# Two attentions with the order of TensorE's work turned round in every other step

## The reference

```
def chunk_attention(q, k, v, rel_bias):          # "second attention", a == 1; head size 64
    ...
        s = jnp.einsum('bqhd,bkhd->bhqk', qch, kb, preferred_element_type=jnp.float32) * scale + bias[None]
        s = jnp.where(valid[None, None, None, :], s, NEG_INF)
        p = jax.nn.softmax(s, axis=-1).astype(vb.dtype)
        return jnp.einsum('bhqk,bkhd->bqhd', p, vb)

def mla_attention(q, k, v):                      # "third attention", a == 2; query and key size 96, value size 64
    ...
        s = jnp.einsum('bqhd,bkhd->bhqk', qi, k, preferred_element_type=jnp.float32) * scale
        s = jnp.where(mask[None, None], s, NEG_INF)
        p = jax.nn.softmax(s, axis=-1).astype(v.dtype)
        return jnp.einsum('bhqk,bkhd->bqhd', p, v)

    x = x + g_a[:, None, :] * jnp.dot(jnp.concatenate([o_mla, o_ca], axis=-1), w_out[l])
```

## Time and profile before

| | |
|---|---|
| median of 3 runs | 1185.09 us (1184.55 to 1185.25) |
| the profiled execution | 1185.58 us, of which the span from the first to the last instruction is 1183.9 us |
| PE busy | 1175.9 us, 99% of the span |
| DVE, ACT, POOL busy | 585.2, 507.9, 454.7 us |
| granted TensorE clock | 9 tenths or more in each of the 40 slices |
| second attention, steps 0 to 19 | about 662 to 708 us from the span's start |
| third attention, steps 0 to 19 | about 727 to 780 us |

### The profile page before, as it was taken

How to read it: one execution, slowest core, us unless ns; L and a number is a source line. 1 busy time by engine, 2 the same in 40 slices (tenths; PEclk the granted TensorE clock), 3 DMA queues, 4 the chain that set the end, 5 groups by cost and what they waited for, 6 DMA issues and landing times.

```text
span 1183.9 us, 16147 instructions
## 1 busy us (share of the span) xinstructions
PE 1175.9 (99%) x5972; PEld 962.0 (81%) x5972; DVE 585.2 (49%) x1150; ACT 507.9 (43%) x794; POOL 454.7 (38%) x181
## 2 busy tenths in 40 slices
PE   9999999999999999999999999999999999999998
PEld 7887778988888888888988667689888888888887
DVE  4276455877777774212574567835434334340000
ACT  6452453634434442322646576834534443432110
POOL 6352224344344433444443210314434434434442
PEclk9999999999999999999999999999999999999999
DMA  8233122545554542223341110202222222222222
GB/s 294 96 107 107 37 80 100 201 177 191 213 188 171 208 155 87 96 96 111 135 144 72 54 37 1 68 30 82 107 107 79 98 106 103 74 73 98 98 97 95
DMA packets 27858, 132.38 MB, mean 112 GB/s; under 512 B 3616, under 2 KB 5024, under 8 KB 18976
## 3 DMA queue, kind: packets, MB, share of 16 engines
q1 hardware_dynamic: 25920, 129.48, 30.5%
q10 hardware_dynamic: 1888, 2.23, 0.6%
HBM read 129.60 MB, written 2.10 MB: 111 GB/s over the span
## 4 chain that ended last, share of the span: by engine, by line
PE 97%; DVE 1%; ACT 1%; DMA 1%; POOL 0%; issue 0%; SPq 0%; DVEq 0%
PE psum L1520 87%; PE psum L1601 2%; PE psum L1589 2%; PE psum L2021 1%; PE psum L1935 1%; PE psum L1834 1%; PE psum L1957 1%; DMA raw<-stream 1%; POOL wl L482 0%; ACT prob L682 0%; DVE prob L1215 0%; PE psum L1799 0%; PE psum L1965 0%; DVE prob L1233 0%; ACT probT L671 0%
## 5 line engine op out<-in xcount | busy, mean ns | idle before, releaser
L466 POOL TENSOR_TENSOR wl<-raw,wh 128x2048 fp32r<-128x2048 f32 (+2 forms) x89 | 365.9, 4111 | 510.5 <-ACT wh L605 285.1
L1520 PE MATMUL psum<-xh,wh 128*128 128x512 f32 (+1 forms) x1032 | 392.7, 381 | 1.3 <-POOL wl L520 1.2
L1520 PE MATMUL psum<-xl,wh 128*128 128x512 f32 (+1 forms) x1032 | 388.0, 376 | 0.0
L1520 PE MATMUL psum<-xh,wl 128*128 128x512 f32 (+1 forms) x1032 | 388.0, 376 | 0.0
L1520 PEld LDWEIGHTS psum<-xh,wh 128*128 128x128 f32 x1032 | 194.0, 188 | 43.1 <-issue 3.5
L1166 DVE SCALAR_TENSOR_TENSOR scratch<-psum,cols,scratch 128x511 f32<-128x511 f32 (+1 forms) x176 | 131.7, 748 | 196.2 <-ACT scratch L743 187.9
L1520 PEld LDWEIGHTS psum<-xh,wl 128*128 128x128 f32 x1032 | 194.1, 188 | 35.2
L1520 PEld LDWEIGHTS psum<-xl,wh 128*128 128x128 f32 x1032 | 194.2, 188 | 35.0 <-issue 0.2
L605 ACT ACTIVATE wh<-raw 128x2048 fp32r<-128x2048 f32 (+1 forms) x50 | 88.4, 1767 | 246.5 <-PE psum L1520 246.5
L1520 PE MATMUL psum<-acth,wh 128*128 128x512 f32 (+1 forms) x374 | 141.0, 377 | 0.0
L1520 PE MATMUL psum<-actl,wh 128*128 128x512 f32 (+1 forms) x374 | 140.8, 377 | 0.0
(11 more groups left out here) (256 smaller groups left out, 1365.3 us busy)
## 6 DMA issues: line engine op xcount, KB each, us to landing
raw<-stream SPq DMA_DIRECT2D x69, 1024.0 KB, 4.7
ada_raw<-ada SPq DMA_DIRECT2D x48, 512.0 KB, 5.4
raw<-down SPq DMA_DIRECT2D x32, 704.0 KB, 4.1
h<-xT SPq DMA_DIRECT2D x8, 256.0 KB, 6.4
outT<-h SPq DMA_DIRECT2D x8, 256.0 KB, 5.1
raw<-stream SPq DMA_DIRECT2D x7, 256.0 KB, 6.7
rel<-rel_tiles ACTq DMA_DIRECT2D x1, 1344.0 KB, 9.5
raw<-stream SPq DMA_DIRECT2D x2, 512.0 KB, 3.9
```

The costliest lines, as they stand in the source:

```text
L466: pool.tensor_tensor(wl[slot][:, 0:w], raw[slot][:, 0:w], wh[slot][:, 0:w].bitcast(F32), ALU.subtract).then_inc(lo_done, 1)
L1520: ins = pe.matmul(out, lhs[a], rhs[b], start=first and n == 0, stop=last and n == 2)
```

## The change

The first attention (`a == 0`) keeps its order and lags. In the second and third:

- PE runs even steps, and steps from 16 on, as before: scores, beside, transposes, values. Odd steps below 16 run values, beside, transposes, scores.
- Values come five steps behind (`LATE`), and step 19 runs the last two of them.
- DVE's norms come two steps behind in place of one. ACT's exponentials come one step behind in place of none.
- There is a third `probT` buffer, in the room of `sq2`, which is now only used outside the loops' steady part.
- The wait for `p2.dve` of 2 moves from the scores of step 3 to the work beside step 3, and the heads are taken out one step later.

```diff
+            with ExitStack() as s2:
+                sq2 = [sb(f"sq2{b}", [P, T], F32, s2) for b in range(2)]
+            probT2.append(sb("probT22", [P, 2, T], F32, s))
...
-        NORM_LAG = 1
         TURN_LAG = 3
         LAG = 4
+        LATE = 5
...
+        def values_of(a, step):
+
+            if a == 0:
+                return [step - LAG] if step >= LAG else []
+            if step == STEPS + LAG - 1:
+                return [STEPS - 2, STEPS - 1]
+            return [step - LATE] if step >= LATE else []
...
@@ ACT: attend @@
+                    buffers = len(probT)
+                    if V >= buffers:
+                        act.wait_ge(att.pv, V - buffers + 1)
+                    act.activation(probT[V % buffers][:, :, 0:w], TURN_BANKS[:, :, 0:w], ACT.Copy).then_inc(att.ptc, 1)
...
+                exp_lag = 0 if a == 0 else 1
                 for step in range(STEPS + LAG):
                     if TURN_LAG <= step < STEPS + TURN_LAG:
                         turned(step)
-                    if step < STEPS:
-                        V, w = unit(a, step), width(step)
+                    if exp_lag <= step < STEPS + exp_lag:
+                        x = step - exp_lag
+                        V, w = unit(a, x), width(x)
...
@@ DVE: attend @@
+                norm_lag = 1 if a == 0 else 2
...
-                    norming = NORM_LAG <= step < STEPS + NORM_LAG
+                    norming = norm_lag <= step < STEPS + norm_lag
                     if norming:
-                        v = step - NORM_LAG
+                        v = step - norm_lag
...
@@ PE: attend @@
+                for step in range(STEPS + LAG):
+                    if a == 0 or step % 2 == 0 or step >= STEPS:
+                        scores_step(step)
+                        if beside is not None:
+                            beside(step)
+                        turn_step(step)
+                        values_step(step)
+                    else:
+                        values_step(step)
+                        if beside is not None:
+                            beside(step)
+                        turn_step(step)
+                        scores_step(step)
```

More of the change, by code:

```diff
@@ L1561, in attend @@
             def attend(a, ready, scores, decays, v, prob, probT, ident, beside=None):
[L1562 to L1572, removed]
-                        for e in range(2):
[L1574 to L1592, removed]
@@ new lines, in scores_step @@
+                def scores_step(step):
+                    if step >= STEPS:
+                        return
+                    V, p, i, w = unit(a, step), step // TB, step % TB, width(step)
+                    outs = scores_banks(a, V)
+                    ready(step)
+                    if a == 0 and step:
+                        pe.wait_ge(att.max, 2 * V - 1)
+                    elif a == 1 and step >= 2:
+                        pe.wait_ge(att.max, 2 * V - 2)
+                    elif step >= 2:
+                        pe.wait_ge(att.raw, 2 * step - 2)
+                    for e in range(2):
+                        ins = scores(p, i, e, outs[e], w)
+                        if decays is None:
+                            ins.then_inc(att.qk, 1)
+                    if decays is not None:
+                        for e in range(2):
+                            decays(p, e, outs[e], w).then_inc(att.qk, 1)
@@ new lines, in turn_step @@
+                def turn_step(step):
+                    if not TURN_LAG <= step < STEPS + TURN_LAG:
+                        return
+                    V, i = unit(a, step - TURN_LAG), (step - TURN_LAG) % TB
+                    pe.wait_ge(att.norm, 2 * V + 2)
+                    if V >= 1:
+                        pe.wait_ge(att.ptc, V)
+                    for e in range(2):
+                        for j in range(i + 1):
+                            ins = pe.transpose(TURN_BANKS[:, e, P * j:P * j + P], prob[V % 4][:, e, P * j:P * j + P], ident[:, :])
+                    ins.then_inc(att.pt, 1)
@@ L1593, in attend, with values_step @@
+                def values_step(step):
+                    for x in values_of(a, step):
+                        V, p, i = unit(a, x), x // TB, x % TB
                         pe.wait_ge(att.ptc, V + 1)
[L1594 removed]
+                        if a == 1 and x == 0:
                             pe.wait_ge(att.max, 2 * unit(1, TB - 1) + 1)
```

28 lines of the change are left out of this document (13 added, 15 removed).

## The result

| | before | after |
|---|---|---|
| median of 6 runs, us | 1185.05 (1184.55 to 1185.28) | 1212.01 (1211.18 to 1212.61) |
| ratio | 1 | 1.0229 [1.0218, 1.0239] |
| span of the profiled execution, us | 1183.9 | 1210.4 |
| second attention, us | 44.94 | 59.96 |
| between second and third, us | 19.90 | 19.90 |

The kernel is 27 us slower. That is the sign of the forecast, but 9 us above its 1203 and 2 us outside its range. What lies between the attentions, and the 404.3 us behind them, took the same time in both, so all of the loss is in the two loops: 15.0 us in the second and 12.2 in the third, less 0.55 us by which the second now starts earlier.

What follows compares the result with a forecast made beforehand. PE, busy 1175.9 of 1183.9 us, was taken as the bound. Terms summed to +10.9 us in the second attention and +7.6 in the third, +18.5 on the median of 1185.1: 1203 us, range 1193 to 1210 (8 in 10).

Steps and rivals of the forecast that it cites:

- Saved shape changes: PE, both attentions: touching groups of the same shape lose their fixed cost, 2.3 us in the second, 2.1 in the third.
- Norms behind the reductions of a late score: Mainly even steps: PE's transposes wait for VectorE's norms, 12.8 us in the second attention, 6.4 in the third.
- The start of the third loop: First transposes of the third attention find VectorE only just begun, which costs 1.3 us.
- the first half of a score isn't ready early: Second attention: both halves end together; if one came earlier, seven waits would shrink by about half a microsecond, 3.5 us.
- The pair of heads: Four steps: from 8.5 us to 11 to 11.5 in the second attention, from 10.85 to 11 to 13 in the third.
- Norms under GpSimd: Norms slowed beside GpSimd's subtractions, charged at half: 0.6 us in the second attention, 3.2 in the third; bounds 0 and 7.5.
- odd steps' transposes: Odd steps: transposes' wait for norms costed at nothing, covered by two groups of values and one of transposes, 1.8 us or more.
- rival 4: PE's clock falls to 1.2 GHz through the second attention's 28 us: some +15, 1218 us; chance 0.06.
- 1: Both attentions: the gain is kept and VectorE is never late, 1179 us; chance 0.06.
- 2: Third attention's narrower waits and starts vanish and its norms miss GpSimd: +11, 1196 us; chance 0.1.
- 3: A wash: waits a third of those found, time within 2 us; chance 0.03.

Runs made afterwards that it cites:

- e10: Changed kernel plus useless 256-column products on PE ahead of even steps' wait for norms, in both attentions: 1208.67 us.
- e3: Changed kernel with VectorE's reciprocal and norms of step - 2 moved ahead of the step's reductions, in both attentions: 1190.0 us.
- e7: Changed kernel with GpSimd's low parts of three weight chunks cut to a 32nd of their columns, the rest not computed: 1203.28 us.
- e6: Changed kernel plus useless 512-column products on PE ahead of even steps' wait for norms, in both attentions: 1220.0 us.
- e8: Changed kernel with both the useless 512-column products on PE and GpSimd's low parts of three chunks cut to a 32nd: 1216.02 us.
- e9: Kernel before the change with GpSimd's low parts of the same three chunks cut to a 32nd, as a control: 1184.48 us.
- e4: Changed kernel with the third attention put back to its old order, lags and values, so only the second is changed: 1198.97 us.
- e12: Changed kernel with norms ahead of the reductions and GpSimd's low parts of three chunks cut to a 32nd: 1184.46 us.

## Why the forecast's sign was right and its size wrong

**What bounds the kernel** was read rightly: PE alone. VectorE and ScalarE were busy for the same time before and after, and 27 us came from PE's idle time and clock.

**Saved shape changes, -4.4.** Seen, and a little small. S512 and S128 together take 1.28 (693.19 to 694.47 in e10) against 1.06 + 0.42 = 1.48 in the earlier trace rows; twenty values take 1.27 to 1.31 against 1.39 from the same rows' prices, so 0.1 where I had 0.16. That is 0.3 per two steps, where I had 0.37.

**Norms behind the reductions of a late score, +12.8 and +6.4.** Right in cause and place, and in the second attention in size. The second attention has 13.2 us in seven waits, the typical ones 2.01 and 1.33 (forecast 2.1 and 1.4); 0.9 of the 13.2 is GpSimd's, in the wait of 2.95. e3 shows the cause: with the norms ahead, 2.6 us of these waits are left in the second attention, and 22 of the 27 us go, the clock's share among them. In the third they are 1.2 and 0.3 where nothing else disturbs (e7), a little under 1.4 and 0.6.

**The start of the third loop, +1.3,** was right: waits of 0.85 (before 747.50) and 0.41 us (before 753.85) in e7. The rule that the first half of a score isn't ready early in the second attention held: VectorE starts 1.27 behind the scores.

**The pair of heads in the second attention** takes 11.31 us where neither the clock nor GpSimd disturbs it (685.19 to 696.50 in e7), inside the forecast's 11 to 11.5. In the kernel after it takes 13.0 (672.95 to 685.95), with both. The third's, forecast at 11 to 13, takes 11.3 in e7 (763.97 to 775.27) and 15.4 in the kernel after (767.14 to 782.54).

**Norms under GpSimd, +0.6 and +3.2: mis-sized in the third.** I had charged half, on the ground that only some of the norms would meet a stretch. The collisions aren't spread by chance. A quarter chunk's split by ScalarE comes at a fixed place in the step and GpSimd follows it at once, so four quarters start together with the norms, twice in the third attention, and reach both an even and an odd step. The second measured 0.9. The third measured 5.4 to 7.1, about the whole of the upper bound there (six norms by 1.1, 6.6). That odd steps' transposes could be costed at nothing was wrong for the same reason, and cost 3.7 us (e6 against e8): the cover that I counted, two groups of values and one of transposes, is gone when three norms take 4.3 us.

**The clock, rival 4, at a chance of 0.06: this is the step that failed.** I took it as all or nothing, 28 us at half speed for some +15, and so as unlikely. What happened lies between all and nothing: behind some of the waits, though not behind all of the same length, the clock fell to half for some 3.4 us, in five places in all. The mean granted clock of the kernel after is 0.991 to 0.994 in all six executions, where the kernel before has 1.00. It cost 4.1 us in the second attention (e10 against after) and up to 3.4 in the third. The forecast's sum had no term for it: a rival at 0.06 stands beside the sum and moves it by nothing.

**The sum.** In the second +10.9 became 10.95 and the clock 4.1. That the first two agree to 0.05 is luck in part: the waits without GpSimd are 12.2 for 12.8, GpSimd 0.9 for 0.6 and the savings smaller. In the third +7.6 became 12.15: 4.4 for waits, start and savings (e7 against e9 is 5.6 with one stretch at half clock of up to 1.7, so 3.9 to 5.6), 5.4 to 7.1 for GpSimd and what remains for the clock. Clock and GpSimd are the two terms over my 1203, the clock the larger (4.1 in the second attention alone, against 2.2 to 3.9 for GpSimd over its 3.2), and of the two only GpSimd was in the range: its upper end had the collisions at their bound (1209), and no clock. With the clock's 4.1 us as an addition to it, not as a rival, the range would have held 1212. The sum itself is 1185.1 + 18.5 = 1203.6; rounding it down to 1203 took off another 0.6.

**Rivals.** 1, 2 and 3 fell: the waits before the transposes of the fourteen even steps come to 19.8 us, 1.4 for each and not 0.3, and the third attention lost 12 us. The second alone (e4) cost 14 us.

**What stays open:** how the third attention's loss of 12.15 us divides between GpSimd and the clock, beyond these bounds and the estimate from the waits; why a wait of 2.01 us brings the clock down in one place and not in another; filling just the waits in front of which the clock falls there was not tried, nor an order of the quarter splits that keeps clear of the norms in the third.

## What to carry to other kernels

When an engine's order is turned round, find the instructions of the other engines that stand behind its now late result in their own in-order programs; here the transposes needed two norms that stood behind two reductions, and moving them ahead gave back 22 of 27 us. Before slack is spent, list what had been hiding in it (here GpSimd's stretches, worth 0.7 us with slack and 8.7 without, the clock's share in that included), and let a new wait of 2 us on TensorE count for more than itself, since the clock can halve behind it. Against 0.3 us per two steps of saved shape changes there is no room for any of these.

## What the runs showed of the hardware

- TensorE's granted clock fell to half (1.2 GHz) for 3.4 to 3.5 us behind waits of 2.01 us (before 672.95) and 2.95 us (before 685.95), in stretches where PE had work before and behind them. The length of the wait alone does not decide it: 2.01 us before 698.83 and 2.02 before 786.46 left the clock at 1.00, and so did two of 1.91 us in e3 (before 751.04 and 762.53) and those of 1.3 us (before 679.00 and 692.82). In e12 it fell at 733.5, behind sixteen one-column products and within a wait of 0.85 us; in e3 the same products and wait (before 734.70) left it at 1.00. The Trainium skill ("TensorE: Matmul & The Clock Gate", "Part 1: The HAM clock gate") says that how busy PE has been sets the clock; these rows agree as far as each fall came in or behind a wait, at waits shorter than I had thought of.
- VectorE's scalings took 1.29 to 1.51 us, whatever their width from 256 to 512 (1.37 for a 128-wide one), while GpSimd subtracted 512-wide quarters of 1.3 us each, against 0.35 to 0.49 alone. Beside 256-wide quarters of 0.72 us they took 0.81 to 0.96 (684.34, 685.08 and 686.42 in the kernel after). A 128x2 multiplication went from 0.16 to 0.62 (767.56 in the kernel after). The Trainium skill's exclusive lock ("SBUF — State Buffer", "SBUF: two separate sides"), which I had weighed and then halved, gave the right size in the third attention.
- A 512-column float32 product takes 0.86 us in its two records (e6, four in 3.5 us), and a group of scores costs nothing fixed when the one before has the same shape (1.28 for a 512-wide and a 128-wide score together, against 1.48).
